# A retention, convolution and expert layer: another order of taps, outputs, state updates and output weights within a head

## What is computed

```python
h = x @ w_in + b_in
q, k, v, g, u_a, u_b, m_r, m_c = jnp.split(h, SPLITS, axis=-1)
q = _rope(q...); k = _rope(k...) * RET_DK ** -0.5
# per head, per chunk
att = einsum(q, k) * dmask
o = att @ v + (q * q_dec) @ s
s_new = exp(c * log_g) * s + (k * k_dec)^T @ v
o = _headnorm(o)
ret_out = (silu(g) * o) @ w_ret_o
u = u_a * sigmoid(u_b)
c = causal depthwise convolution of [conv_buf, u], width 31, + conv_b
c = silu(_layernorm(c))
mixed = (sigmoid(m_r) * ret_out + sigmoid(m_c) * (c @ w_conv_o + b_conv_o)) @ w_out
x = _layernorm(alpha * x + mixed)
```

## Time and profile before

| | us |
|---|---|
| median of 3 runs | 1326.45 |
| lowest, highest | 1325.32, 1327.02 |
| the profiled execution, its own time | 1327.39 |
| its span in the profile | 1325.5 |
| PE busy | 1132.7 (85%) |
| DVE busy | 970.4 (73%) |
| ACT busy | 637.4 (48%) |
| POOL busy | 126.1 (10%) |
| second head, first matmul to next head's first | 154.5 to 277.7 |
| last expert stage, from | about 720 |

### The profile page before, as it was taken

How to read it: one execution, slowest core, us unless ns; L and a number is a source line. 1 busy time by engine, 2 the same in 40 slices (tenths; PEclk the granted TensorE clock), 3 DMA queues, 4 the chain that set the end, 5 groups by cost and what they waited for, 6 DMA issues and landing times.

```text
span 1325.5 us, 15143 instructions
## 1 busy us (share of the span) xinstructions
PE 1132.7 (85%) x5825; PEld 882.4 (67%) x5825; DVE 970.4 (73%) x1021; ACT 637.4 (48%) x581; POOL 126.1 (10%) x224
## 2 busy tenths in 40 slices
PE   3994998599679949999843999999999999999960
PEld 3982886398459828999642767676767767666740
DVE  3597679577866977346462888888888888888846
ACT  2440333043214412462222777777777777777740
POOL 3120120102011202100002000000000000000012
PEclk9996999599879978999955999999999999999985
DMA  8563474447436633733525999999999999999934
GB/s 193 189 219 120 164 242 157 159 151 241 143 143 209 232 123 136 212 128 129 193 92 202 340 377 369 381 379 380 381 381 380 381 381 380 381 381 380 387 102 109
DMA packets 171371, 332.24 MB, mean 251 GB/s; under 512 B 8474, under 2 KB 45642, under 8 KB 171280
## 3 DMA queue, kind: packets, MB, share of 16 engines
q1 hardware_dynamic: 150704, 264.41, 56.9%
q0 software_dynamic: 20592, 66.81, 14.8%
HBM read 295.28 MB, written 36.63 MB: 250 GB/s over the span
## 4 chain that ended last, share of the span: by engine, by line
PE 74%; DVE 16%; DMA 3%; issue 2%; ACT 2%; POOL 1%; SPq 0%; POOLq 0%; DVEq 0%; ACTq 0%
PE bank L721 69%; DVE cT L1324 6%; PE bank L762 3%; DVE st L1421 2%; DVE lo L1045 2%; PE bank L950 2%; DMA x_in<-in_x_prompt_dram 1%; DVE o_tok L1415 1%; DMA x_slots<-x,slot 1%; DVE stats L1406 1%; POOL x_slots L678 1%; DMA y_back<-y_slots,slot 1%; DMA y_slots<-yo 1%; POOL y_back L706 0%; ACT cT L1146 0%
## 5 line engine op out<-in xcount | busy, mean ns | idle before, releaser
L1572 DVE TENSOR_TENSOR mlo<-mraw,mhi 128x2048 fp32r<-128x2048 f32 x192 | 439.5, 2290 | 78.6 <-ACT mhi L1197 75.4
L1197 ACT ACTIVATE mhi<-mraw 128x2048 fp32r<-128x2048 f32 x192 | 367.4, 1914 | 93.6 <-PE bank L721 83.5
L721 PE MATMUL bank<-mhi,xg_hi 128*96 128x512 f32 x512 | 203.2, 397 | 1.4 <-DVE xg_lo L1577 1.4
L721 PE MATMUL bank<-mhi,xg_lo 128*96 128x512 f32 x512 | 203.0, 397 | 0.0
L721 PE MATMUL bank<-mlo,xg_hi 128*96 128x512 f32 x512 | 201.6, 394 | 0.0
L1045 DVE TENSOR_TENSOR lo<-raw,hi 128x2048 fp32r<-128x2048 f32 x56 | 128.2, 2290 | 82.9 <-ACT hi L1040 41.1
L1040 ACT ACTIVATE hi<-raw 128x2048 fp32r<-128x2048 f32 x47 | 90.0, 1914 | 175.3 <-PE bank L721 175.3
L721 PE MATMUL bank<-xT_hi,hi 128*128 128x336 f32 x512 | 165.6, 323 | 6.4 <-DVE lo L1045 6.4
L721 PE MATMUL bank<-xT_hi,lo 128*128 128x336 f32 x512 | 163.5, 319 | 0.0
L721 PE MATMUL bank<-xT_lo,hi 128*128 128x336 f32 x512 | 163.2, 319 | 0.0
L1324 DVE SCALAR_TENSOR_TENSOR cT<-W,hv,cT 128x336 f32<-128x336 f32 x240 | 136.1, 567 | 6.9
(11 more groups left out here) (248 smaller groups left out, 1526.0 us busy)
## 6 DMA issues: line engine op xcount, KB each, us to landing
mraw<-in_w_gate_dram SPq DMA_DIRECT2D x64, 1024.0 KB, 11.1
mraw<-in_w_up_dram SPq DMA_DIRECT2D x64, 1024.0 KB, 11.0
mraw<-in_w_down_dram SPq DMA_DIRECT2D x64, 1024.0 KB, 11.7
raw<-in_w_in_dram SPq DMA_DIRECT2D x40, 1024.0 KB, 5.3
st<-in_state_ret_dram POOLq DMA_DIRECT2D x32, 512.0 KB, 4.7
out_dram<-st POOLq DMA_DIRECT2D x32, 512.0 KB, 4.5
raw<-in_w_ret_o_dram SPq DMA_DIRECT2D x8, 1024.0 KB, 6.0
x_slots<-zeros POOLq DMA_DIRECT2D x12, 512.0 KB, 4.9
```

The costliest lines, as they stand in the source:

```text
L721: i = pe.matmul(out, a, b, start=s, stop=e)
L1197: act.activation(mhi[:, v % MH, :], mraw[:, v % MR, :], ACT.Copy).then_inc(mhi_ready, 1)
L1572: dve.tensor_tensor(mlo[:, v % MH, :], mraw[:, v % MR, :], mhi[:, v % MH, :].bitcast(f32), ALU.subtract).then_inc(mlo_ready, 1)
```

## The change

All of it lies in the loop over heads; the arithmetic of each result stays the same, but for the order of the work.

- **Taps.** `conv(h, w0, w1)` does tap w for both channel blocks in turn, so that a tap waits for the one before the one in front of it. The 31 pairs are spread anew: two behind unit 4, six behind qdiag, four around the v tiles, four around the third score group, six between units 8 and 9, one behind the statistics, and the last eight in the next head: six behind its unit 1, two behind its unit 2 (for the last head behind the gates' first two units). A new semaphore `taps_done` lets ACT overwrite the windows.
- **Outputs.** PE computes o2, o1, o0; DVE takes statistics of 2 and 1 together, then of 0; turns, gating and high and low parts follow in the order 2, 1, 0. `ps0` and `ps1` stand between and behind the turns. On DVE `moments` is the statistics up to the reciprocal, `normal` the normalisation into `o_tok`, `gated` the product with the gate, `sg_low` its low part. The gated outputs stay in `rt`, and `sg_f` is gone.
- **State updates.** The four sets go in between wr0 | wr1, wr2 | wr3, wr4 | wr5, wr6 | wr7, with DVE's additions to match; the sets are taken by sequences 0 to 3 with both halves, then 4 to 7 (the order of sets was the same before).
- **Buffers.** The copies of a head's vectors (`hv`, `hs`) are gone, read in place instead; `v_lo` gets a place of its own over `sub`, where the low outputs shared it before.

```diff
-        hs = sb("hs", [128, HS])
+        v_lo = nc.alloc_sbuf_tensor_at("v_lo", [TT, DV], f32r, offset=base[0])
...
+        def strips(n):
+
+            return [c + 4 * (n // 2) for c in range(4)], n % 2
+
+        def strip_names(n):
+            seqs_, p = strips(n)
+            return [f"Pst{b}{p}" for b in seqs_]
+
         PRE = Stage(None, [f"Pxt{i}" for i in range(6)] + ["Pvec", "Pbqk", "Pvec2"])
         HEAD = Stage(PRE, ["Fub0", "Fub1", "Fua0", "Fua1", "Phist0", "Phist1", "Fq0", "Fq1", "Fk0", "Fk1",
                            "PuS", "PuP", "-vp0", "-vp1", "-vp2", "Pv0", "Pv1", "Pv2", "Pkt0", "Pkt1",
-                           "Patt0", "Patt1", "Fg0", "Fg1", "Patt2", "Fg2", "Fg3", "Po0", "Po1", "Po2"]
-                     + [f"Pst{c + 4 * r}{p}" for r in range(2) for p in range(2) for c in range(4)]
-                     + [f"PoT{i}" for i in range(NT)] + ["Pps0", "Pps1"] + [f"Fwr{m}" for m in range(8)], H)
+                           "Patt0", "Patt1", "Fg0", "Fg1", "Patt2", "Fg2", "Fg3", "Po2", "Po1", "Po0",
+                           "PoT2", "PoT1", "Pps0", "PoT0", "Pps1"]
+                     + ["Fwr0"] + strip_names(0) + ["Fwr1", "Fwr2"] + strip_names(1) + ["Fwr3", "Fwr4"] + strip_names(2)
+                     + ["Fwr5", "Fwr6"] + strip_names(3) + ["Fwr7"], H)
...
-                for t in range(NT):
+                for t in (2, 1, 0):
...
+                def o_turn(t):
+                    pe.wait_ge(evac[HEAD.bank[f"o{t}"]], HEAD.used(f"o{t}", h) + 1)
+                    b = bank[HEAD.bank[f"oT{t}"]]
+                    turn(HEAD, f"oT{t}", h, [(b[:, j * TT:(j + 1) * TT], o_tok[:, t, j * 128:(j + 1) * 128], TT) for j in range(4)])
+
+                def prompt_state(p):
+                    name = f"ps{p}"
+                    room(HEAD, name, h)
+                    group(HEAD, name, h, [(bank[HEAD.bank[name]][:, :], kdp[:, t, p * 128:(p + 1) * 128], v_tok[:, t, :], t == 0, t == NT - 1) for t in range(NT)])
+
+                def update(n):
+
+                    mine, p = strips(n)
+                    cols = slice(p * 128, (p + 1) * 128)
+                    for b in mine:
+                        room(HEAD, f"st{b}{p}", h)
+                    for k, (a, v) in enumerate(((kds_hi, v_hi), (kds_hi, v_lo), (kds_lo, v_hi))):
+                        for b in mine:
+                            rows = slice(32 * (b % 4), min(32 * (b % 4) + 32, TT))
+                            i = pe.matmul(bank[HEAD.bank[f"st{b}{p}"]][:, :], a[rows, b // 4, cols], v[rows, :], start=k == 0, stop=k == 2)
+                            if k == 2:
+                                i.then_inc(group_done, 1)
+
+                def wr(m):
+                    f_group(HEAD, f"wr{m}", h, T_view(hi, m // 4), T_view(lo, m // 4), slice(m % 4 * 128, (m % 4 + 1) * 128), sg_hi, sg_lo, 4)
+
+                o_turn(2)
+                o_turn(1)
                 pe.wait_ge(evac[HEAD.bank["kt0"]], HEAD.used("kt0", h) + 1)
                 pe.wait_ge(evac[HEAD.bank["kt1"]], HEAD.used("kt1", h) + 1)
                 alone(pe, waits_met)
...
+                prompt_state(0)
+                o_turn(0)
+                prompt_state(1)
...
+                split_ready(U_HEAD, 8, h)
+                wr(0)
+                pe.wait_ge(vlo_ready, h + 1)
+                alone(pe, waits_met)
+                update(0)
+                wr(1)
+                wr(2)
+                update(1)
+                wr(3)
+                split_ready(U_HEAD, 9, h)
+                wr(4)
+                update(2)
+                wr(5)
+                wr(6)
+                update(3)
+                wr(7)
...
+                if h:
+                    for c in range(2):
+                        act.wait_ge(*took(HEAD, f"ua{c}", h - 1))
...
+                if h:
+                    act.wait_ge(taps_done, h)
...
-                for n, tt in enumerate((slice(0, 2), slice(2, 3))):
+                for n, tt in enumerate((slice(1, 3), slice(0, 1))):
...
+                sg_high(2)
+                sg_high(1)
+                prompt_out(0)
+                sg_high(0)
+                prompt_out(1)
...
+            def conv(h, w0, w1):
+
                 for w in range(w0, w1):
-                    tap = hv[:, VCW + c * CW + w:VCW + c * CW + w + 1]
-                    src = windows(c)[:, :, w:w + NI]
-                    if w == 0:
-                        ins = dve.tensor_scalar(out, src, tap, hv[:, VCB + c:VCB + c + 1], ALU.mult, ALU.add)
-                    else:
-                        dve.wait_ge(dve_step, conv_last[0])
-                        ins = dve.scalar_tensor_tensor(out, src, tap, out, ALU.mult, ALU.add)
-                    conv_last[0] = count(ins)
+                    for c in range(2):
+                        out = cT[:, h * 2 + c, :].rearrange("p (n i) -> p n i", i=NI)
+                        tap = vec[:, h, VCW + c * CW + w:VCW + c * CW + w + 1]
+                        src = windows(c)[:, :, w:w + NI]
+                        if w == 0:
+                            ins = dve.tensor_scalar(out, src, tap, vec[:, h, VCB + c:VCB + c + 1], ALU.mult, ALU.add)
+                        else:
+                            dve.wait_ge(dve_step, conv_last[c])
+                            ins = dve.scalar_tensor_tensor(out, src, tap, out, ALU.mult, ALU.add)
+                        conv_last[c] = count(ins)
                 if w1 == CW:
-                    dve.wait_ge(dve_step, conv_last[0])
+                    for c in range(2):
+                        dve.wait_ge(dve_step, conv_last[c])
+                    dve.sem_inc(taps_done, 1)
...
-                dve.tensor_copy(hv[:, :], vec[:, ds(h, 1), :].rearrange("p a n -> p (a n)")).then_inc(hv_ready, 1)
-                dve.tensor_copy(hs[:, :], tab[:, ds(h * HS + TB["heads"][0], HS)]).then_inc(hv_ready, 1)
-                dve.wait_ge(hv_ready, h * 2 + 2)
-                for u in (1, 2):
-                    L(U_HEAD, u, h)
+                hv = vec[:, h, :]
+                hs = tab[:, TB["heads"][0] + h * HS:TB["heads"][0] + (h + 1) * HS]
+                L(U_HEAD, 1, h)
+                if h:
+                    conv(h - 1, 23, 29)
+                L(U_HEAD, 2, h)
+                if h:
+                    conv(h - 1, 29, CW)
...
+                    if n == 0:
+                        dve.wait_ge(windows_ready, h * 2 + 2)
+                        conv(h, 0, 2)
...
-                    dve.wait_ge(*took(HEAD, f"hist{c}", h))
-                    dve.wait_ge(*took(HEAD, f"ua{c}", h))
-                dve.wait_ge(windows_ready, h * 2 + 2)
-
-                conv(0, h, 0, 12)
+                conv(h, 2, 8)
                 L(U_HEAD, 6, h)
                 dve.wait_ge(vb_full, h * 16 + 16)
                 for t in range(NT):
                     b, e = full(HEAD, f"v{t}", h)
                     dve.tensor_tensor(v_tok[:, t, :], b[0:TT, :], vb[:, :], ALU.add).then_inc(e, 1)
-                dve.wait_ge(*took(HEAD, "v0", h))
-                dve.sem_inc(v_ready, 1)
-                conv(0, h, 12, 18)
+                    if t == 0:
+                        conv(h, 8, 9)
+                    elif t == 1:
+                        conv(h, 9, 11)
+                    else:
+                        dve.wait_ge(*took(HEAD, "v0", h))
+                        dve.sem_inc(v_ready, 1)
+                conv(h, 11, 12)
                 L(U_HEAD, 7, h)
...
-                conv(0, h, 18, 23)
+                conv(h, 12, 15)
                 decayed(2)
-                conv(0, h, 23, CW)
+                conv(h, 15, 16)
                 L(U_HEAD, 8, h)
-                conv(1, h, 0, 15)
+                conv(h, 16, 22)
                 L(U_HEAD, 9, h)
...
+                moments((2, 1), slice(1, 3))
+                conv(h, 22, 23)
+                dve.wait_ge(rstd_done, h * 2 + 1)
+                normal(2)
+                normal(1)
+                moments((0,), slice(0, 1))
                 for m in range(4):
                     dve.wait_ge(*took(HEAD, f"g{m}", h))
+                gated(2)
+                gated(1)
+                dve.wait_ge(rstd_done, h * 2 + 2)
+                normal(0)
+                sg_low(0, 2)
+                sg_low(1, 1)
+                gated(0)
+                sg_low(2, 0)
...
-                for m in range(8):
-                    b, e = full(HEAD, f"wr{m}", h)
-                    dve.tensor_tensor(retT[:, m, :], b[:, 0:T], retT[:, m, :], ALU.add).then_inc(e, 1)
-                    conv(1, h, 15 + 2 * m, min(17 + 2 * m, CW))
-                    if m == 4:
-                        L(U_HEAD, 10, h)
...
+                add_ret(0)
+                new_state(0)
+                add_ret(1, 2)
+                new_state(1)
+                add_ret(3, 4)
+                L(U_HEAD, 10, h)
+                new_state(2)
+                add_ret(5, 6)
+                new_state(3)
+                add_ret(7)
                 dve.wait_ge(*took(HEAD, "wr7", h))
 
```

(7 more changed lines are left out.)

## The result

| | before | after |
|---|---|---|
| median, us | 1326.74 (4 runs, 1325.32 to 1328.70) | 1240.43 (4 runs, 1239.67 to 1240.83) |
| the profiled execution, its own time | 1327.39 | 1240.83 |
| its span | 1325.5 | 1238.6 |
| PE busy | 1132.7 (85%) | 1119.7 (90%) |
| second head | 123.2 | 101.1 |

What follows compares the result with a forecast made beforehand. PE is fullest but idles about 19 us a head, awaiting normalised outputs and state additions. A head sums 65.0 + 9.05 + 0.25 + 7.3 + 15.0 + 4.9 = 101.5 us; four save 87, giving 1240, range 1233 to 1254.

Steps and rivals of the forecast that it cites:

- Sum for a head: One head's stretches on PE added up: 101.5 us against 123.2, 21.7 less.
- The total: Whole kernel: four heads at 21.7 us less, 87 us, giving 1240 us; chance 0.65.
- An update at full clock: PE's state update among the wr groups: not in the trace, taken as 1.0 us, bounds 0.83 and 1.66.
- Taps: DVE's convolution taps, alternating between two channel blocks: 0.485 us a tap instead of 0.604.
- Rival A: Alternating DVE's taps gives nothing, they stay at 0.604 us: 11 us dearer, 1251; chance 0.11.
- Statistics at +70: DVE's output statistics start about 70 us from a head's start instead of 77.
- the walk: DVE's new order followed with traced durations up to the statistics: they start at 224.4, 7.0 us earlier.
- Rival B: DVE falls behind among the updates; updates 1 and 2 each wait 1 us: 8 us more, 1248; chance 0.09.
- Carried taps: Eight tap pairs at the next head's start on DVE: nothing on PE moves, cover 0.7 us.
- Rival C: Next head's history load lands late behind stores: 3 us in three heads, 1249; chance 0.06.
- The mean: After the last head, carried taps finish at +14.3, PE arrives at +14.8: free by 0.5 us.
- Rival D: PE's clock falls behind the outputs and stays at 1.2 GHz to the head's end: 1333 us; chance 0.03.

Runs made afterwards that it cites:

- four more pairs: Changed kernel with four more tap pairs between the reciprocal and the normalisation, four fewer carried into the next head: 1259.77 us.
- the old tail: Changed kernel's taps with the tail of the kernel before (outputs 0, 1, 2, then updates, turns, prompt states, wr groups): 1304.95 us.
- the block of updates: Changed kernel with the four state updates in one block between the second prompt state and wr0, DVE's additions to match: 1286.49 us.
- late statistics: Changed kernel with nine tap pairs instead of six between units 8 and 9, none behind the statistics, six carried instead of eight: 1253.34 us.

## Why the prediction held, point by point

- **Sum for a head.** Forecast 101.5, measured 101.1. Up to the outputs 65.0 (132.47 to 197.45), as taken. Outputs 8.9 (9.05). Idle 0.35 (0.25). Turns and prompt states 6.7 (7.3): from start to start the three turns take 1.5 (1.65) and the prompt states 5.2 (5.5). The stretch of wr groups and updates 20.2 (19.9): the updates with the last one's wait took 4.3 (4.9), but the wr groups 15.9 (15.0), about 0.1 us more at each of the eight hand-overs between groups and updates. No term was off by more than 0.9, and they partly cancel. (277.7 - 262.6 is 15.1 and not 15.2; nothing hangs on it. The 3.7 us between updates 0 and 1 run from the end of one to the start of the next, the 4.7 between 1 and 2 from start to start; both measured 4.8 from start to start.)
- **The total.** That 1240 meets 1240.43 so closely is in part luck. The heads won 0.4 us each more than forecast, 4 x 22.1 = 88 us, and the profiled executions lie only 86.6 apart: the first head's normalisation comes only 6.0 us earlier (110.59 to 104.63) where the second's statistics come 7.0 earlier in their head, and 0.7 us more went behind the last one. The two deviations cancel.
- **An update at full clock** was the one unknown price, taken at 1.0 between 0.83 and 1.66. It costs 0.90 from its start to the next group's.
- **Taps.** Twelve in 5.83 us: (5.83 - 0.567) / 11 = 0.478, against 0.485. Rival A's 0.604 is what the run without alternation shows; its price, 11 us, was measured at 9, but not by its path: PE waited 1.2 us more in a head and not 2.4, and a fallen clock in two heads made up for most of that. The two numbers are close by luck.
- **Statistics at +70** came at +69.9. The waits that the walk had for ScalarE and the third score group are in the trace at 0.1 to 1.1 us (0.2 to 1.2 in the walk).
- **Rival B**, updates 1 and 2 waiting: they do not. The wait is at update 3 alone, as worked out, 0.73 for 0.9. The run without carried taps shows how the mechanism would look.
- **Carried taps.** Unit 1's low half ends at +4.6, the taps at +14.5, where I had +4.4 and +14.3. But unit 3's low half starts at +19.7, not at +17.05. ScalarE waits 7.7 us for its load, which takes 13.0 us from issue to landing (12.9 without alternation), in the stretch in which the stores run; that they are what delays it was not tried by itself. The low half is done at +22.0 and PE needs it at about +22.6, so this cost nothing, but the cover is down to some 0.6 us. The prediction took all loads to come earlier with the low halves; this one's data came later.
- **Rival C, the history.** It is issued 2.6 us after the border (3.5 forecast), behind five stores:

```profile
233.06 2.51 POOL L613 DMA_DIRECT2D out_dram<-st  x4 [7.85 <-DVE st L1501]
235.58 0.53 POOL L639 DMA_DIRECT2D out_dram<-ps_out  x1
236.22 0.81 POOL L592 DMA_DIRECT2D hist<-in_state_conv_dram  x1
```

  It takes 9.5 us to land, where it took 4.0 before (the view of DMA issues, second head's start), so it is there at about +12, and PE turns it at +14.9 without a wait. My 11 us ran from the issue and left out the transfer's own time among the stores; under 3 us are left.
- **The mean** after the last head: PE works from 433.91 on in one piece of 48.17 us in the chain. Free, as said.
- **Rival D**, slower by clock, was wrong in its mechanism, not only unlikely. It had the low clock last to the head's end, as it did from 231 to 258. But there the updates kept PE waiting. With four more pairs the clock falls in every head and is back at 1.00 by 218, 4 us after PE has taken up work that doesn't break off, for 0.9 us a head instead of 23. With the old tail it stays low longer, as before, behind updates that wait (the new taps with the old tail, and the block of updates).
- **Where the gain came from**, in steps of the runs: alternation alone -14, the rest of the taps' new places 7 more (-21), turns and prompt states ahead of the updates, and the outputs' new order, 18 more (-39), updates between the wr groups 46 more (-85). These are differences of medians and sum to the 85 us that separate 1325.7 from 1240.43. The order in which parts are taken matters: alternation is worth 9 in the changed kernel and 14 in the old one.

## What to carry to other kernels

When two engines hand banks back and forth, put the other engine's independent work between the hand-overs: in each head three waits of 2.9 us went to one of 0.7, and the 9.7 us for the normalised outputs to 0.35, without any instruction of DVE becoming shorter. Before cutting work on the engine that is late, see what PE could do meanwhile; the faster taps alone brought 14 to 21 of the 86 us. For a chain of dependent short operations on DVE, two chains in turn make each step 0.126 us cheaper here.

## What the runs showed of the hardware

- In these runs a wait of PE of up to 1.3 us cost itself and no clock, and longer ones could cost more. At 1.6, 2.6 and 2.7 us the granted clock fell to 1.2 GHz in some heads and stayed at 2.4 in others of the same run, behind waits of the same length, for 1.4 to 1.7 us extra; at 4.2 it fell in all, for 0.9. The spread may come from it, which isn't shown: with late statistics or nothing carried the times of one kernel lie 7 us apart, with waits up to 1.3 us at most 3.4; but without alternation they lie only 2 apart, and with four more pairs 5, though the profiled heads are alike there. What decides from head to head is not settled by these runs.
- A dependent tap on DVE starts 0.604 us after the one it waits for, and 0.478 us after its neighbour with an independent one in between, for the same instruction of 0.567 us.
- A load of 240 KB behind 2.5 MB of stores took 9.5 us to land instead of 4.0, and the first 1 MB weight load issued in that stretch 13.0, where the four there have a median of 7.6. Which of the transfers beside it slows it was not tried.
